# Attention of the first mixer in 24 steps instead of 32: two query blocks, or two head pairs, in one step

## What is computed

```python
qa, ka, va, qb, kb, vb, qi, ki, wi, ga, gb = split(rmsnorm(x) @ w_in)
o_a = _mixer_a(qa, ka, va, rel_bias)      # branch one: 8 heads of 64, causal by chunks of 64, plus a relative bias
o_b = _mixer_b(qb, kb, vb, qi, ki, wi)    # branch two: 8 query heads, 2 key heads; each query keeps its 128 best keys
merged = sigmoid(ga) * (o_a @ w_branch_a) + sigmoid(gb) * (o_b @ w_branch_b)
x = x + merged @ w_out
```

## Time and profile before

| | |
|---|---|
| median of three runs | 2096.61 us (2095.94 to 2097.45) |
| the profiled execution, by its own time | 2096.84 us |
| its span, first to last instruction | 2095.0 us |
| TensorE busy in the span | 2077.4 us (99%) |
| VectorE, ScalarE, GpSimd busy | 37%, 37%, 41% |
| attention of the first mixer | from 428.9 to 662.9 us of the span |

### The profile page before, as it was taken

How to read it: one execution, slowest core, us unless ns; L and a number is a source line. 1 busy time by engine, 2 the same in 40 slices (tenths; PEclk the granted TensorE clock), 3 DMA queues, 4 the chain that set the end, 5 groups by cost and what they waited for, 6 DMA issues and landing times.

```text
span 2095.0 us, 26431 instructions
## 1 busy us (share of the span) xinstructions
PE 2077.4 (99%) x9502; PEld 1678.5 (80%) x9502; DVE 780.4 (37%) x1280; ACT 766.7 (37%) x1058; POOL 851.5 (41%) x360
## 2 busy tenths in 40 slices
PE   8999999999999999999999999999999999999999
PEld 6888888777777888888888888888777778888887
DVE  5222211657853432222215222211588864222200
ACT  5222322344344442223323333223577754223221
POOL 2444545333322444444444444454322244444443
PEclk9999999999999999999999999999999999999999
DMA  4223233322221322332232322232444432332332
GB/s 168 97 100 100 98 103 108 135 71 71 71 71 51 101 92 99 100 100 95 96 120 90 100 90 91 100 115 97 121 121 121 120 112 90 100 100 90 111 103 78
DMA packets 64254, 209.36 MB, mean 100 GB/s; under 512 B 7936, under 2 KB 8960, under 8 KB 64192
## 3 DMA queue, kind: packets, MB, share of 16 engines
q1 hardware_dynamic: 62784, 205.75, 30.3%
q10 hardware_dynamic: 1408, 2.78, 0.4%
HBM read 193.69 MB, written 2.10 MB: 93 GB/s over the span
## 4 chain that ended last, share of the span: by engine, by line
PE 89%; DVE 6%; ACT 3%; issue 1%; DMA 0%; SPq 0%; DVEq 0%; ACTq 0%
PE ps L431 28%; PE ps L433 28%; PE ps L432 28%; DVE sb_s L1511 2%; DVE sb_e L1566 1%; PE ps L587 1%; PE ps L598 1%; DVE sb_s L1513 1%; ACT sb_e L1119 1%; DVE sb_w L1503 1%; ACT sb_e L1117 1%; PE ps L633 1%; DVE scratch L1182 1%; ACT sb_e L1115 0%; PE ps L531 0%
## 5 line engine op out<-in xcount | busy, mean ns | idle before, releaser
L394 POOL TENSOR_TENSOR w_lo<-raw,w_hi 128x1024 fp32r<-128x1024 f32 x356 | 851.3, 2403 | 1224.7 <-ACT w_hi L875 1120.7
L431 PE MATMUL ps<-xn_hi,w_hi 128*128 128x512 f32 x1912 | 755.8, 395 | 8.1 <-DVE xn_lo L1211 7.9
L433 PE MATMUL ps<-xn_hi,w_lo 128*128 128x512 f32 x1912 | 746.0, 390 | 0.0
L432 PE MATMUL ps<-xn_lo,w_hi 128*128 128x512 f32 x1912 | 745.5, 390 | 0.0
L431 PEld LDWEIGHTS ps<-xn_hi,w_hi 128*128 128x128 f32 x1912 | 359.7, 188 | 90.1 <-issue 8.8
L875 ACT ACTIVATE w_hi<-raw 128x1024 fp32r<-128x1024 f32 x360 | 366.6, 1048 | 150.9 <-PE ps L433 118.9
L433 PEld LDWEIGHTS ps<-xn_hi,w_lo 128*128 128x128 f32 x1912 | 359.6, 188 | 76.2
L432 PEld LDWEIGHTS ps<-xn_lo,w_hi 128*128 128x128 f32 x1912 | 360.0, 188 | 73.7 <-issue 1.2
L1179 DVE TENSOR_TENSOR scratch<-ps,rstd 128x512 f32<-128x512 f32 x200 | 137.6, 690 | 580.2 <-PE ps L433 579.8
L432 PE MATMUL ps<-h_lo,w_hi 128*128 128x512 f32 x704 | 273.9, 389 | 0.0
L431 PE MATMUL ps<-h_hi,w_hi 128*128 128x512 f32 x704 | 273.9, 389 | 0.0
(11 more groups left out here) (179 smaller groups left out, 1413.1 us busy)
## 6 DMA issues: line engine op xcount, KB each, us to landing
raw<-weights SPq DMA_DIRECT2D x360, 512.0 KB, 3.4
k_hi_twice<-sb_k_hi SPq DMA_DIRECT2D x32, 128.0 KB, 2.3
k_lo_twice<-sb_k_lo SPq DMA_DIRECT2D x32, 128.0 KB, 2.3
x_sb<-x_t SPq DMA_DIRECT2D x8, 256.0 KB, 5.8
bias<-rel ACTq DMA_DIRECT2D x1, 2048.0 KB, 10.4
q_both<-sb_q_hi SPq DMA_DIRECT2D x16, 128.0 KB, 2.2
q_both<-sb_q_lo SPq DMA_DIRECT2D x16, 128.0 KB, 2.3
out_t<-x_sb SPq DMA_DIRECT2D x7, 256.0 KB, 4.5
```

The lines of the kernel that those rows point to most:

```text
L394: nc.gpsimd.tensor_tensor(w_lo[s][:, :, :], raw[s][:, :, :], w_hi[s][:, :, :].bitcast(F32), ALU.subtract).then_inc(S["lo_done"], 1)
L431: pe.matmul(to, w_hi[s][:, k, :], hi, start=opens, stop=False)
L432: pe.matmul(to, w_hi[s][:, k, :], lo, start=False, stop=False)
L433: last = pe.matmul(to, w_lo[s][:, k, :], hi, start=False, stop=ends)
```

## The change

Branch one keeps its order of pairs, but a pair now has three steps for four: block 1; blocks 0 and 2 together; block 3. Blocks 0 and 2 have 128 and 384 columns and fill one bank of 512 side by side. In branch two the blocks 0 and 1 take two pairs of heads in a step (2 x 128 and 2 x 256 columns), blocks 2 and 3 one as before. That makes 12 + 12 steps. `FIRST[m]` counts the parts (block and pair) ahead of step m, and `parts(m)` yields those of step m with their columns. Search rounds per step go from two to three. The same 120 and 128 pieces of units are shared out over fewer steps: in branch one 10 a step for 7.5, later about 9.1 for 7.1.

```diff
-TOP_EACH = 2
-STEPS = [(0, i, c) for c in range(4) for i in range(QT)] + [(1, i, c) for i in range(QT) for c in range(4)]
-HALF = len(STEPS) // 2
+TOP_EACH = 3
+STEPS = [[(0, i, c) for i in blocks] for c in range(4) for blocks in ((1,), (0, 2), (3,))]
+HALF = len(STEPS)
+STEPS += [[(1, i, c) for c in pairs] for i in range(2) for pairs in ((0, 1), (2, 3))]
+STEPS += [[(1, i, c)] for i in range(2, QT) for c in range(4)]
+FIRST = list(itertools.accumulate((len(step) for step in STEPS), initial=0))
+def parts(m):
+    at = 0
+    for n, (br, i, c) in enumerate(STEPS[m]):
+        yield FIRST[m] + n, br, i, c, slice(at, at + P * (i + 1))
+        at += P * (i + 1)
...
         def turn_weights(n):
+            for a in range(2):
-                pe.wait_ge(S["p_normed"], 2 * n + a + 1)
+                pe.wait_ge(S["p_normed"], 2 * FIRST[n + 1] - 1 + a)
                 if n:
                     pe.wait_ge(S["pt_copied"], 2 * n - 1 + a)
-                for j in range(i + 1):
+                for j in range(width(n) // P):
...
         def copy_turned(m):
                 act.wait_ge(S["p_turned"], 2 * m - 1 + a)
                 if br == 0:
-                    dst, src = p_all[:, a, 0:i + 1, P * i:W], PS[:, 6 + a, 0:W].rearrange("p (j n) -> p j n", n=P)
+                    for _, _, i, _, cols in parts(m - 1):
+                        last = copy(p_all[:, a, 0:i + 1, P * i:P * (i + 1)],
+                                    PS[:, 6 + a, cols].rearrange("p (j n) -> p j n", n=P))
...
         def add_bias(m):
-            for a in range(2):
-                add = bias[:, 2 * c + a, W - 1::-1] if br == 0 else mask[i][:, :]
-                dve.wait_ge(S["s_done"], 2 * m + a + 1)
+            for n, br, i, c, cols in parts(m):
+                for a in range(2):
+                    add = bias[:, 2 * c + a, P * (i + 1) - 1::-1] if br == 0 else mask[i][:, :]
+                    dve.wait_ge(S["s_done"], 2 * FIRST[m + 1] - 1 + a)
...
         def normalise(m):
-            dve.wait_ge(S["p_made"], 2 * m + 2)
+            dve.wait_ge(S["p_made"], 2 * FIRST[m + 1])
-            nc.vector.reciprocal(inv, row_sum[:, 2 * m:2 * m + 2]).then_inc(S["inv_made"], 1)
+            nc.vector.reciprocal(inv, row_sum[:, sums]).then_inc(S["inv_made"], 1)
```

More of the change, by code:

```diff
@@ L615, in weigh_values @@
         def weigh_values(n):
[L617 to L621, removed]
+            if n < HALF:
+                if n in GROUP_LAST:
+                    weigh_branch_a(GROUP_LAST.index(n))
                 return
             pe.wait_ge(S["pt_copied"], 2 * n + 2)
-            if e == 0:
-                if group >= 2:
+            for _, br, i, c, part in parts(n):
+                group = QT + i
+                if c == 0:
                     pe.wait_ge(S["o_lo_done"], group - 1)
[L627 to L634, removed]
+                    pe.wait_ge(S["v_copied"], QT + 1)
+                for j in range(i + 1):
+                    for a in range(2):
+                        h = HEADS_OF[br][c][a]
+                        cols, to = slice(HD * a, HD * a + HD), slice(HD * (h % 2), HD * (h % 2) + HD)
+                        at, turned_at = P * (h // 2), part.start + P * j
+                        last = pe.matmul(PS[to, group % 2, at:at + P], vb[:, j, cols],
+                                         p_t[:, a, turned_at:turned_at + P], start=(j == 0), stop=(j == i))
             last.then_inc(S["pv_done"], 1)
@@ L1037, in attention_1 @@
                 if m < len(STEPS):
[L1038 to L1044, removed]
+                    for n, _, _, _, cols in parts(m):
+                        for a in range(2):
+                            p = scratch[:, 2 * (m % 2) + a, cols]
+                            one = slice(2 * n + a, 2 * n + a + 1)
+                            act.wait_ge(S["s_biased"], 2 * n + a + 1)
+                            nc.scalar.activation(p, p, ACT.Exp, bias=row_neg_max[:, one], scale=-1.0,
+                                                 accum_out=row_sum[:, one]).then_inc(S["p_made"], 1)
                 if 1 <= m < HALF:
@@ L1416, in normalise @@
+            nc.vector.reciprocal(inv, row_sum[:, sums]).then_inc(S["inv_made"], 1)
             dve.wait_ge(S["inv_made"], m + 1)
-            for a in range(2):
-                p = scratch[:, 2 * (m % 2) + a, 0:W]
-                nc.vector.tensor_scalar(p, p, inv[:, a:a + 1], None, ALU.mult).then_inc(S["p_normed"], 1)
+            for n, _, _, _, cols in parts(m):
+                for a in range(2):
+                    p, one = scratch[:, 2 * (m % 2) + a, cols], 2 * (n - FIRST[m]) + a
+                    nc.vector.tensor_scalar(p, p, inv[:, one:one + 1], None, ALU.mult).then_inc(S["p_normed"], 1)
```

76 lines of the change are left out of this document (39 added, 37 removed).

## The result

The changed kernel takes 2101.56 us (median of 10 executions, 2101.21 to 2102.69), the kernel before beside it 2096.55 us: 5.0 us more, ratio 1.0026, 95% interval 1.0018 to 1.0034. That is slower than forecast (2098.2) and beyond the range's upper end of 2100.7. The profiled execution took 2102.25 us, 0.7 us above the median.

What follows compares the result with a forecast made beforehand. TensorE was taken as the bound, busy 2077.4 of 2095.0 us. The terms -2.1 - 0.4 + 2.2 + 1.3 + 0.6 = +1.6 us on the median 2096.61 gave 2098.2 us, range 2094.9 to 2100.7.

Steps and rivals of the forecast that it cites:

- fewer visits of TensorE: Both branches: eight score interruptions at 0.20 us and four value product visits at 0.15 go, plus starting transposes; -2.1 us.
- the old wait of step 12: Step 12, branch two: TensorE's wait for ScalarE's copy before a value transpose goes, values being turned in step 9; -0.4 us.
- wait in step 8: Branch one's third value transpose waits for copies of step 7's weights, GpSimd delaying the add in k's leave; +2.2 us.
- steps 11 to 13: VectorE falls behind from step 10, so TensorE waits in step 12 for q's last leave to free its bank; +1.3 us.
- what is late next: Step 12's bias behind q's leave, then three rounds and a gate per step until step 15; 0 to 1.0, taken +0.6 us.
- the sign of being wrong: The forecast counts as wrong if the waits add to more than 6 us or VectorE keeps up in step 8.
- Rival 2: VectorE's backlog does not clear in steps 12 to 15, each transpose waiting about a microsecond; 2102.2 us, chance 0.06.
- rival 3: GpSimd holds up scalings in two or three of the steps with four scalings; 2101.2 us, chance 0.05.
- The range's upper bound: Upper bounds of the three waits with the visits' gain, -2.1 + 2.2 + 2.0 + 1.0 = +3.1, and a microsecond of backlog: 2100.7 us.

Runs made afterwards that it cites:

- one_only: Changed kernel with branch two in 16 single steps as before and two search rounds per step; 2097.90 us, ratio 1.0008 to the kernel before.
- two_only: Changed kernel with branch one in 16 single steps as before and two search rounds per step; 2094.80 us, ratio 0.9994 to the kernel before.
- late_block: Changed kernel with step 8's wait for ScalarE's copies and the turning of branch one's third value block both behind the projection unit's last piece; 2098.26 us.
- lock_rounds: Changed kernel with the edits of no_lock and rounds together, step 8 left as it is; 2095.45 us.
- no_lock: Changed kernel, but in steps 12 to 16 ScalarE rounds the next gate unit only after VectorE's scalings of the step before; 2098.68 us.
- rounds: Changed kernel with two search rounds for three in nine steps (7, 10, 11, 12 and 14 to 18); 2096.82 us.
- kb_free: Changed kernel, but in step 8 the gate unit's rounding stands behind ScalarE's exponentials and copies, so GpSimd is idle during the key block's add; 2099.52 us.
- late_turn: Changed kernel with only the transposes of branch one's third value block moved to step 8's end, the wait for copies left in place; 2101.48 us.

## Why the prediction was wrong

The sum against what the traces show, in its order:

| term | predicted | measured | from |
|---|---|---|---|
| fewer visits of TensorE | -2.1 | -3.9 | one_only, two_only |
| the old wait of step 12 | -0.4 | -0.4 | gone from the view |
| wait in step 8 | +2.2 | +2.1 | 507.21 to 509.56 |
| half clock behind it | none | +1.6 | 5.20 for 3.61 us; late_block |
| steps 11 to 13 | +1.3 | +1.8 | rows of step 12, scores of step 13 |
| what is late next | +0.6 | +3.9 | rows of steps 14 to 16 |
| sum | +1.6 | +5.1 | stage 239.54 to 244.73, +5.2 |

lock_rounds checks the two rows of steps 11 to 16 together: without them its stage is 5.8 us shorter, for 1.8 + 3.9. The waits of the view add to 6.3 us, over the 6 that I had named as the sign of being wrong.

**The step that failed is "what is late next", taken as +0.6.** I bounded it with 0 to 1.0 us by setting three rounds and a gate beside a step of about 8.6 us. Rival 2 named the point from which it decides, VectorE's 8.3 to 8.9 us a step against TensorE's 8.6, and rival 3 the block on the scalings; both got small chances as if they were independent. They are one mechanism. VectorE, late by its third round, does the mask late; ScalarE's exponentials end late, and the rounding of the next unit, whose slot TensorE has left by then, follows them at once (572.04); GpSimd starts 0.78 us after the first scaling and the fourth has to wait for its whole run. The 2.13 us that this costs make VectorE's cycle 11.01 us; without them it is 8.87 (no_lock), just under TensorE's 9.05. So with the hold-up it starts the next step later still: its mask comes 5.7 us after the scores in step 14 and 8.0 in step 15 (572.58 to 580.60). two_only shows the loop open (the same joined steps in branch two, VectorE in time, no meeting). no_lock takes the meeting away and leaves VectorE late; rounds leaves the meeting and takes part of the lateness away; with both, TensorE waits for nothing in branch two. "None of those rows in the trace was held up" was true of before, and said nothing on a case in which ScalarE comes late and four scalings stand for two.

**Missing was the half clock.** I priced a wait of 2.2 us by its own length. late_block, which removes only that wait, gives 3.74 us of stage and 3.3 of the median. A row that could have warned me was not there: before shows no wait of that length followed by half clock.

**The visits were worth nearly twice what I gave.** I counted no gain in the scores, since as many matmuls remain. But the fixed part belongs to a visit, not to a matmul. Before, four matmuls over 512 columns each take 1.06 us (640.20 to the first of these rows); in the changed kernel eight over 256 columns take 1.07 for the same 2048 columns (the other two):

```profile
641.26 1.10 PE L598 MATMUL ps<-const,scratch 128*128 128x128 f32 x8
...
563.86 1.14 PE L607 MATMUL ps<-kb,qb 64*128 64x256 f32 x8
564.93 0.44 PE L617 MATMUL ps<-const,scratch 128*128 128x128 f32 x2
```

2048 columns at 2.4 per ns are 0.85, so 0.21 us is fixed in both, and four over 128 columns before have it too (513.65 to 514.07, 0.42 us for 0.21 of columns); eight visits fewer are 1.7 us that my sum lacked. Without this error the miss would have been larger: 1.8 us too little gain against 5.3 us too little loss.

**Right were** the wait of step 8 in place, size and cause (the add of kb held by GpSimd: kb_free takes 0.9 us of it away, the rest is the chain itself), the wait of step 12 for the leave of q, the old wait's end, and that the searches are done in time. In the size of step 8 two errors cancel: the leave started 0.6 us after the scores, not 0.2, and lasted 3.5 us, not 4.0. In the chain of steps 11 to 13 the bias of step 11 came 4.3 us after its scores (534.95 to 539.21), not 4.9, and TensorE waited 1.2 us for the leave behind it; the rest of the 1.8 are slow starts and the scalings of step 12. The range's upper bound (+3.1) leaves out the -0.4 that the sum has; with it the range would have ended at 2100.3. The Trainium skill's page SBUF — State Buffer, section Who interferes with whom, has in the same place a second rule that I did not use: a tensor_scalar may run in a mode that takes both port pairs, and then contends with GpSimd too, whoever comes second waiting for the whole instruction. The traces agree with the waiting: the fourth scaling, which starts 0.02 us after GpSimd, takes 2.48 us for 0.35, and three that started before GpSimd were not held. In which mode the scalings ran no run here shows.

## What to carry to other kernels

Joining steps pays what the visits of the bound engine cost (here 0.2 us each for scores and for the return to the stream, 0.15 for a value product), but it also makes lumps on the engines beside it, and a lump is paid where the reserve of a step, not of the stretch, is used up: compute each helper engine's cycle of a joined step with every hold-up in it, and don't give two rivals separate chances where one brings the other about. Where a helper engine follows another's end (rounding behind exponentials), ask what a late arrival makes coincide. And look for the cheap repairs before giving a change up: the same joined steps with one round fewer in nine of them, two reorderings and a later value block went from 2101.6 to 2092.8 us.

## What was unexpected of the hardware

A wait of 2.1 us in a TensorE that is otherwise dense was followed by about three microseconds at 1.2 GHz in the changed kernel, no_lock, rounds, late_turn and lock_rounds, and not in the profiled execution of one_only, with the same wait of 2.0 us in the same place. With 1.1 us left of it (kb_free) the profiled execution had none in the stage. The kernels have a second such place in the second block: the profiled execution of the changed kernel shows 2.05 us of waiting at 1541 us and the scores behind it slow, before has 2.10 us at 1537 and they run at full speed:

```profile
1541.41 0.77 PE L733 MATMUL ps<-k_hi_twice,q_both 128*128 128x512 f32 x1 [2.05 <-DVE sb_s L1532]
1541.98 0.63 PE L733 MATMUL ps<-k_lo_twice,q_both 128*128 128x512 f32 x1
```

```profile
1537.14 0.47 PE L715 MATMUL ps<-k_hi_twice,q_both 128*128 128x512 f32 x1 [2.10 <-DVE sb_s L1513]
1537.45 0.39 PE L715 MATMUL ps<-k_lo_twice,q_both 128*128 128x512 f32 x1
```

The first of those takes 0.57 us to the next start, the second 0.31. In the profiled execution of late_block, whose stage is at full clock, this second place has the half clock too. What decides it from one execution to the next stays open; none of the runs varied it alone.
